# Forgetting attention by pairs of heads on the two halves of TensorE's array

## The reference, cut to what matters

```
q, g = split(h @ w_qg);  q = q * 64 ** -0.5
logits = einsum('bqhd,bkhd->bhqk', q_block, k) + (c_q - c_k)   # float32
logits = where(key_pos <= query_pos, logits, -inf)
p = softmax(logits);  o = einsum('bhqk,bkhd->bqhd', p, v)
y = (o * sigmoid(g)) @ w_out
```

## Time and profile before

| | us |
|---|---|
| median of 3 runs | 2778.18 |
| lowest, highest | 2772.0, 2779.1 |
| profiled execution | 2774.4 |
| its span | 2772.6 |
| PE busy in it | 2685.2 (97%) |
| DVE, ACT, POOL busy | 1536.2, 1021.2, 98.6 |

### The profile page before, as it was taken

The page is one execution under the profiler, slowest core; times in us unless marked ns, Lnnn a source line. Parts: engine busy times, 40 slices in busy tenths (PEclk is TensorE's granted clock), DMA queues, the critical chain, the costliest instruction groups (busy, mean ns, idle before and its releaser), DMA issues. The chain is left out here.

```text
span 2772.6 us, 31166 instructions
## 1 busy us (share of the span) xinstructions
PE 2685.2 (97%) x12382; PEld 2094.1 (76%) x12382; DVE 1536.2 (55%) x2570; ACT 1021.2 (37%) x1588; POOL 98.6 (4%) x124
## 2 busy tenths in 40 slices
PE   8999999999999999999998999999999998999998
PEld 6787688887976656888876876688887765788886
DVE  5455676776255554747465255466653898433432
ACT  4344443334234444434245334323223213322322
POOL 0000000000000000000000000011100110000000
PEclk9999999999999999999999999999999999999999
DMA  5323235542221112333324210266642111233231
GB/s 167 102 81 94 78 119 162 167 149 88 70 85 46 39 46 61 103 95 95 96 69 135 84 61 9 94 194 194 193 146 82 54 46 38 76 99 99 93 98 46
DMA packets 283495, 266.84 MB, mean 96 GB/s; under 512 B 13283, under 2 KB 268567, under 8 KB 283351
## 3 DMA queue, kind: packets, MB, share of 16 engines
q1 hardware_dynamic: 266919, 210.33, 24.7%
q0 software_dynamic: 15024, 54.33, 6.7%
q10 hardware_dynamic: 1408, 0.20, 0.0%
HBM read 262.72 MB, written 2.10 MB: 96 GB/s over the span
## 5 line engine op out<-in xcount | busy, mean ns | idle before, releaser
L481 DVE TENSOR_TENSOR w_lo<-raw,w_hi 128x1024 fp32r<-128x1024 f32 x396 | 482.9, 1224 | 745.8 <-ACT w_hi L476 744.9
L2145 PE MATMUL G<-H_hi,w_hi 128*128 128x512 f32 (+1 forms) x2016 | 812.1, 403 | 15.1 <-DVE H_lo L357 7.9
L476 ACT ACTIVATE w_hi<-raw 128x1024 fp32r<-128x1024 f32 x396 | 417.0, 1056 | 1019.6 <-PE G L2145 911.5
L2145 PE MATMUL G<-H_hi,w_lo 128*128 128x512 f32 (+1 forms) x2016 | 786.4, 390 | 0.0
L2145 PE MATMUL G<-H_lo,w_hi 128*128 128x512 f32 (+1 forms) x2016 | 786.1, 390 | 0.0
L2145 PEld LDWEIGHTS G<-H_hi,w_hi 128*128 128x128 f32 x2016 | 381.3, 189 | 133.9 <-issue 53.2
L2145 PEld LDWEIGHTS G<-H_lo,w_hi 128*128 128x128 f32 x2016 | 381.5, 189 | 83.7 <-issue 9.1
L2145 PEld LDWEIGHTS G<-H_hi,w_lo 128*128 128x128 f32 x2016 | 380.9, 189 | 80.0
L2145 PE MATMUL G<-hid_hi,w_hi 128*128 128x512 f32 x864 | 343.4, 397 | 4.7 <-DVE hid_lo L600 4.7
L2145 PE MATMUL G<-hid_hi,w_lo 128*128 128x512 f32 x864 | 338.1, 391 | 0.0
L2145 PE MATMUL G<-hid_lo,w_hi 128*128 128x512 f32 x864 | 337.9, 391 | 0.0
(11 more groups left out here) (305 smaller groups left out, 2581.5 us busy)
## 6 DMA issues: line engine op xcount, KB each, us to landing
raw<-in_w_ff SPq DMA_DIRECT2D x128, 512.0 KB
mod_w<-in_w_mod POOLq DMA_DIRECT2D x96, 512.0 KB, 4.5
raw<-in_ffn_w_up SPq DMA_DIRECT2D x176, 256.0 KB
raw<-in_ffn_w_down SPq DMA_DIRECT2D x40, 512.0 KB
raw<-in_w_in SPq DMA_DIRECT2D x28, 512.0 KB
raw<-in_mlstm_w_in SPq DMA_DIRECT2D x24, 512.0 KB
raw<-in_kv_w SPq DMA_DIRECT2D x16, 512.0 KB
raw<-in_fox_w_qg SPq DMA_DIRECT2D x16, 512.0 KB
```

Of the source, the lines that this page charges most:

```text
L476: act.activation(w_hi[:, j, :], raw[:, j, :], ACT.Copy).then_inc(hi_done, 1)
L481: dve.tensor_tensor(w_lo[:, j, :], raw[:, j, :], w_hi[:, j, :], ALU.subtract).then_inc(lo_done, 1)
L2145: mm = pe.matmul(G[:, 2 * p + m, 0:n], lw[:, k, ms], rh[:, t, 0:n], start=(t == 0 and q == 0), stop=(t == st["ktiles"] - 1 and q == 2), sk ...
```

## The change

- Two heads (2q and 2q + 1, e = 0 and 1) are worked together: a step n is block b = n % 4 of pair q = n // 4; 32 steps instead of 64.
- `scores(n)`: head e reads partitions 64e to 64e + 63 (as before) and writes bank M0 or M1 by e, not by b. The keys of each head are cut in two pieces (256 + 256 in block 3, 256 + 128 in block 2, 128 + 128 in block 1, one piece in block 0), and the order is piece 0 of head 0, piece 0 of head 1, piece 1 of head 0, piece 1 of head 1. Scores n wait for both logits of step n - 1.
- `values(q)`: the eight products of the pair alternate between the heads, head 0 onto partitions 0 to 63 of M3 and head 1 onto 64 to 127. `output` takes all 128 partitions at once.
- `turn(n, e)` comes two steps behind `scores(n)`; the two of a step have one projection unit between them, and still share bank M2. Scores of the next step stand last in a step.
- Steps 0 to 25 have two projection units each, one at the start and one between the turns. Steps 26 and 27 have none, steps 28 to 31 one unit of `x_out` each, and two more stand between the last turns.
- `row(1)` is issued ahead of the loop; two rows are issued in blocks 0 and 1 of each pair; xN0 holds four rows, both heads are masked in block 3.
- On ACT a step is exponential of head 0, evacuation of head 0 (of step n - 2), exponential of head 1, evacuation of head 1, the row copy, then splits and evacuations of projections. On DVE it is both logits, both scalings of step n - 1, the output, the maskings, then the splits.
- In the diff the three long loops are those of PE, ACT and DVE, in this order.
- The tiles xL, x_row, xN0, xN1 and xPT get new places and packed layouts (only the causal part is held; xPT once instead of twice).

```diff
+        xL = at("xL", 160 * K, [P, 2, 10 * P])
+        xN0 = at("xN0", 176 * K + 128, [P, 4, T])
+        xPT = at("xPT", 188 * K, [P, 24 * P])
...
-            pool.wait_ge(fx["y"], FOX_HEADS)
+            pool.wait_ge(fx["y"], FOX_HEADS // 2)
...
+        FOX_PAIRS = FOX_HEADS // 2
+        FOX_STEPS = TB * FOX_PAIRS
+        WOVEN_STEPS = (8 * 7 - FOX_AHEAD) // 2
+        xl_at = [0, P, 3 * P, 6 * P]
         def units_by(step):
-            return FOX_AHEAD + sum(1 for k in range(8 * 7 - FOX_AHEAD) if 4 * (k // 4) + UNIT_AT[k % 4] <= step)
+            return min(FOX_AHEAD + 2 * (step + 1), 8 * 7)
...
+        def probs(e, b):
+            return xL[:, e, xl_at[b]:xl_at[b] + (b + 1) * P]
+        def turned_probs(e, b):
+            first, pitch = (b * P, 4 * P) if e == 0 else (16 * P - 4 * P * b, 5 * P)
+            return xPT[:, first:first + (b + 1) * pitch].rearrange("p (s m) -> p s m", m=pitch)[:, :, 0:P]
+        def key_probs(e, s):
+            first = 5 * P * s if e == 0 else 5 * P * (3 - s) + (s + 1) * P
+            return xPT[:, first:first + T - s * P]
...
-                if n >= 2:
-                    pe.wait_ge(fx["m"], n - 1)
-                pe.matmul(M[:, b % 2, 0:(b + 1) * P], xQ[hs, h // 2, b * P:b * P + P], xK[hs, h // 2, 0:(b + 1) * P],
-                          start=True, stop=True).then_inc(fx["s"], 1)
+                if n:
+                    pe.wait_ge(fx["m"], 2 * n)
+                half = (b + 1) * HP if b % 2 else (b + 2) // 2 * P
+                for first, end in ((0, half), (half, (b + 1) * P)):
+                    for e in range(2 if end > first else 0):
+                        hs = slice(HP * e, HP * e + HP)
+                        mm = pe.matmul(M[:, e, first:end], xQ[hs, q, b * P:b * P + P], xK[hs, q, first:end],
+                                       start=True, stop=True)
+                mm.then_inc(fx["s"], 1)
...
+                    place = s if e == 0 else b - s
+                    mm = pe.transpose(M[:, 2, place * P:place * P + P], probs(e, b)[:, s * P:s * P + P], ident[:])
...
                 for s in range(TB):
-                    mm = pe.matmul(M[0:HP, 3, s * P:T], xV[:, s, HP * h:HP * h + HP], xPT[h % 2][:, s, s * P:T],
-                                   start=(s == 0), stop=(s == TB - 1), skip_group_check=True)
+                    for e in range(2):
+                        h = 2 * q + e
+                        mm = pe.matmul(M[HP * e:HP * e + HP, 3, s * P:T], xV[:, s, HP * h:HP * h + HP], key_probs(e, s),
+                                       start=(s == 0), stop=(s == TB - 1), skip_group_check=True)
...
+            for n in range(FOX_STEPS):
+                q, b = n // TB, n % TB
+                if n == WOVEN_STEPS:
+                    finish(work)
+                unit(n)
+                if b == 2 and q:
+                    values(q - 1)
+                if n >= 2:
+                    turn(n - 2, 0)
+                unit(n)
+                if n >= 28:
+                    next(outs)
+                if n >= 2:
+                    turn(n - 2, 1)
+                if b < 2 and q < FOX_PAIRS - 1:
+                    row(2 * (q + 1) + b)
+                if n < FOX_STEPS - 1:
+                    scores(n + 1)
+            for n in (FOX_STEPS - 2, FOX_STEPS - 1):
+                for e in range(2):
+                    turn(n, e)
+                    if n < FOX_STEPS - 1:
                         next(outs)
+            values(FOX_PAIRS - 1)
             finish(outs)
...
+            for n in range(FOX_STEPS):
+                q, b = n // TB, n % TB
+                exps(n, 0)
+                if n >= 2:
+                    turned(n - 2, 0)
+                exps(n, 1)
+                if n >= 2:
+                    turned(n - 2, 1)
+                if b < 2 and q < FOX_PAIRS - 1:
+                    row(2 * (q + 1) + b)
+                for _ in range(evacuated_by(n - 1, 3) - taken):
+                    next(work)
+                    taken += 1
+                if n == WOVEN_STEPS:
+                    finish(work)
+                    act.wait_ge(chunk_used, used_after("x_g3"))
+                for t in {26: (0, 1), 27: (2, 3), 28: (4,), 29: (5,)}.get(n, ()):
+                    mixed(t)
...
+            for n in range(FOX_STEPS):
+                q, b = n // TB, n % TB
+                for e in range(2):
+                    logits(n, e)
+                if n:
+                    for e in range(2):
+                        scaled(n - 1, e)
+                if b == 2 and q:
+                    output(q - 1)
+                if b == 3 and q < FOX_PAIRS - 1:
+                    masked(2 * q + 2)
+                    masked(2 * q + 3)
+                for _ in range(evacuated_by(n - 2, 2) - taken):
+                    next(work)
+                    taken += 1
+                if n == WOVEN_STEPS + 1:
+                    finish(work)
+                for t in {27: (0, 1), 28: (2, 3), 29: (4,), 30: (5,)}.get(n, ()):
+                    mixed(t)
```

More of the change, by code:

```diff
@@ new lines, in turned_probs, with scores, turn @@
+        def turned_probs(e, b):
[4 more added lines that the diff above has]
+            return xPT[:, first:first + T - s * P]
+        def fox_pe(pe, linear, linear_units, from_h, squares_behind):
+            def scores(n):
+                q, b = n // TB, n % TB
+                if b == 0 and q % 2 == 0:
+                    wait_read(pe, f"x_q{q // 2}", 0)
+                if n:
+                    pe.wait_ge(fx["m"], 2 * n)
[6 more added lines that the diff above has]
+                mm.then_inc(fx["s"], 1)
+            def turn(n, e):
+                b = n % TB
+                if 2 * n + e:
+                    pe.wait_ge(fx["pt"], 2 * n + e)
+                pe.wait_ge(fx["p"], 2 * n + e + 1)
@@ L1108, in row @@
                     pe.wait_ge(row_c, 5)
-                elif h >= 3:
-                    pe.wait_ge(fx["y"], h - 2)
+                elif h // 2 >= 3:
+                    pe.wait_ge(fx["y"], h // 2 - 2)
                 if h:
@@ L1120, in fox_pe @@
             linear("x_q0", H_hi, H_lo, need=from_h("pre1"))
+            row(1)
             def woven():
@@ L1129, in fox_pe @@
             wait_all_read(pe, "kv_k")
-            scores(0, 0)
+            scores(0)
             next(work)
@@ L1133, in fox_pe, with unit @@
             outs = linear_units("x_out", H_hi, H_lo, need=from_h("fox"), behind=squares_behind("post1"), every=1)
[L1134 to L1151, removed]
-                        next(outs)
[L1153 to L1157, removed]
+            def unit(n):
+                if n < WOVEN_STEPS:
+                    next(work)
[21 more added lines that the diff above has]
+                    if n < FOX_STEPS - 1:
+                        next(outs)
+            values(FOX_PAIRS - 1)
             finish(outs)
@@ L1201, in fox_act, with exps, turned @@
             finish(keys)
[L1203 to L1213, removed]
+            def exps(n, e):
+                b = n % TB
+                act.wait_ge(fx["m"], 2 * n + e + 1)
+                act.activation(probs(e, b), probs(e, b), ACT.Exp, bias=mx[:, b, 2 * e + 1:2 * e + 2], scale=-1.0,
+                               accum_out=rsum[:, b, 2 * e:2 * e + 1]).then_inc(fx["e"], 1)
+            def turned(n, e):
+                q, b = n // TB, n % TB
+                if b == 0 and q:
+                    act.wait_ge(fx["o"], q)
+                act.wait_ge(fx["t"], 2 * n + e + 1)
+                act.activation(turned_probs(e, b), M[:, 2, 0:(b + 1) * P].rearrange("p (s n) -> p s n", n=P),
                                ACT.Copy).then_inc(fx["pt"], 1)
@@ L1232, in fox_act @@
             work, taken = woven(), 0
[L1233 to L1250, removed]
+            for n in range(FOX_STEPS):
+                q, b = n // TB, n % TB
+                exps(n, 0)
[15 more added lines that the diff above has]
+            for e in range(2):
+                turned(FOX_STEPS - 2, e)
             mixed(6)
-            for b in range(1, TB):
-                turned(FOX_HEADS - 1, b)
+            for e in range(2):
+                turned(FOX_STEPS - 1, e)
             mixed(7)
@@ L1323, in scaled, with logits @@
[L1323 to L1327, removed]
+            def logits(n, e):
+                q, b = n // TB, n % TB
+                h, first = 2 * q + e, b * P
+                out, least = probs(e, b), 3.0e38
+                dve.wait_ge(fx["s"], n + 1)
+                if q:
+                    dve.wait_ge(fx["t"], 2 * (n - TB) + e + 1)
+                dve.memset(tok[:, 16 + 4 * e + b:17 + 4 * e + b], 0.0)
+                if b:
+                    link(dve.tensor_tensor_reduce(out[:, 0:first], M[:, e, 0:first], xN0[:, h % 4, 0:first], -1.0, least,
+                                                  ALU.add, ALU.min, mx[:, b, 2 * e:2 * e + 1]))
+                    dve.memset(tok[:, 24 + 4 * e + b:25 + 4 * e + b], 0.0)
```

(33 more changed lines are left out.)

69 lines of the change are left out of this document (25 added, 44 removed).

## The result

| | before | changed |
|---|---|---|
| median of 4 runs each | 2776.68 us | 2738.02 us |
| lowest to highest | 2772.0 to 2779.1 | 2733.85 to 2741.9 |
| profiled execution | 2774.4 us | 2741.9 us |
| its span | 2772.6 us | 2740.1 us |

The ratio is 0.9863, 95% interval 0.9841 to 0.9884: 39 us faster. A second series of the unaltered changed kernel gave 2735.83 (ratio 0.9852, 0.9835 to 0.9868).

A forecast was written before the change was run, and what follows sets the result against it. PE, busy 97% of the span, was taken as the bound. Saving 30.8 us over eight pairs, less 0.6 for waits and 7 at the end, gave 23.2 us off and a median of 2755 us, range 2744 to 2771.

The forecast's parts named there:

- only the second pass of one product overlaps the first of the next: n equal products that alternate take n + 1 pass times: Scores and values on PE: alternating two-pass products of two heads overlap only partly, n + 1 pass times instead of 2n.
- two overlap terms: Per pair of heads, overlap of the halves saves 1.27 us in the scores and 1.71 us in the values.
- Weight loads as a second bound: Scores: if loads can't run beside each other, a pair's streaming takes 3.20 us instead of 2.77; 3.0 was taken.
- The reading of L1422: Products alternating between column halves at 30.9 ns a pass, against 53 alone, were read as two running side by side.
- Turns and projections: PE's transposes and projection products keep their counts; units broken into 8 groups instead of 6 cost 0.1 us a pair.
- Handing over of bank 2: Bank 2 passes to ACT and back within one unit; waits cost 0.1 us a pair, ends 0 and 0.8.
- The end of the attention: From step 26 no unit lies between; some 9.5 idle us against 2.45, so 7 lost, ends 3 and 12.
- the second: Rival: nothing overlaps in scores or values, the end loses less idle time; 2775 us, chance 0.12.
- first: Rival: only column halves overlap, so scores gain only the shape changes; 2765 us, chance 0.15.
- third: Rival: only row halves overlap, exposed value loads eat the values' overlap; 2768 us, chance 0.08.
- the fourth: Rival: the attention's end falls to half clock for all of its 38 us, 12 more; 2767 us, chance 0.06.
- the fifth: Rival: bank 2 becomes the bound, 1.6 us lost in each of 32 steps; slower, 2806 us, chance 0.05.

The follow-up runs named there:

- e1: Changed kernel with both heads of a pair on the same half, so no halves to overlap: 2770.27 us, ratio to before 0.9973.
- e3: Changed kernel with score pieces head by head, both pieces of the first head and then both of the second: 2735.65 us, ratio to before 0.9844.
- e4: Changed kernel with a pair's values head by head, four products of the first and then four of the second: 2747.85 us, ratio to before 0.9891.
- e9: Changed kernel with a pair's values by threes: three products of the first head, three of the second, then one of each: 2749.37 us, one run.
- e10: Changed kernel with a pair's values by twos: two products of the first head, two of the second, then again: 2735.18 us, one run.
- e2: Changed kernel with each head's scores of a step as one product, not cut in two pieces of the keys: 2735.12 us, ratio to before 0.9848.

## Why the prediction was wrong

What bounds the kernel, and that only PE's sum counts, held. So did the terms read from rows: e1 gives 25.13 for a pair without overlap, and 26.54 less my 0.97 for shapes, less the 0.47 found below for turns and projections, is 25.10. The 0.20 once for each group of scores and 0.17 for the values are there unchanged.

The step that failed is "only the second pass of one product overlaps the first of the next: n equal products that alternate take n + 1 pass times". It rested on one assumption, that PE starts passes strictly in order, so that a product's second pass, which waits for its half, also holds up the other head's product behind it. The runs show it wrong: a pass starts as soon as its own half is free if no more than three passes wait ahead of it (`e3`, `e4`, `e9`, `e10`). I also called this counting the bound of the overlap, so that no rival and no sign of being wrong was faster than the forecast. The two overlap terms alone would have made it 2745, at the edge of the range (0.8 + 0.43 a pair, below); the terms of turns, of bank 2 and of the end took it out. By term:

- Scores: I said 3.0 us of streaming in place of 4.27; it is 3.01 - 4 x 0.20 = 2.2. 0.8 a pair too little.
- Values: 2.56 in place of 4.27; it is 2.13. 0.43 too little.
- Weight loads as a second bound (3.20 in the scores): none seen. Twenty-eight loads of 128 columns a pair cost no more than sixteen (`e2` against the changed kernel: 1.06 and 1.07 in the widest step). The Trainium skill's "TensorE: Matmul & The Clock Gate" (Part 3, The mechanism) has the rule that a load overlaps running products only when its row group differs. That doesn't hold in the values here, as I had weighed: both heads' loads are for all rows, and sixteen passes take the 2.30 us of eight. The same section of the Trainium skill also lets a load run ahead into a background weight buffer, which I had left out; the 2.30 us agree with that. The same page's section "Measured speedup vs the span model" gives a pack of tiles the time of one product and some 4 ns for each further one; the 7 ns and the unchanged 2.30 us agree with that, and by it both terms would have come out near what was measured.
- The reading of L1422: I took it as support for my counting. Its mean, 30.9 ns a pass, was no support: in long alternation both countings give the same, and only the ends of a chain differ. Its start could have decided, in the trace before: a narrow window (1503.8 to 1503.9) holds two records, 6 ns apart, where my counting has the second column half wait for the first one's second pass, some 0.1 us later.

```profile
1503.84 0.28 PE L1422 MATMUL G<-rm,sel 128*64 128x64 f32 x2
```

- Turns and projections: I charged 0.1 a pair for two more breaks. The sum of all else, 26.54 - 0.97 - 2.13 - 2.13 = 21.31, leaves 0.47 against 20.84: a gain. Transposes with a projection behind them cost 0.18 less than ahead of scores or a row (0.35 against 0.53), and the projection 0.09 more, four times a pair: 0.36. Summed from start to start over a pair, turns go from 3.04 to 2.28 us and projections from 11.75 to 11.97. I had taken the turns' durations over, without asking how much of them was the change of shape behind them.
- Handing over of bank 2: I took 0.1 a pair, with up to 0.8. No steady turn waits: PE is busy in all of the 20.84 us.

Together 0.8 + 0.43 + 0.57 + 0.1 = 1.9 a pair, 15 over eight pairs. The end of the attention: 7 us lost in my sum, from 2.45 idle to 9.5; it is 6.7 idle (33.10 - 26.39), 4.3 lost. The long stall I put at 4 us is 2.87, at the place and with the releaser I named. The clock at the end: the stretch at half is 6.8 us where there were 10.2; I had let it stand. With 3 for the end and 1 to 2 for the clock, 23 becomes 42 to 43, against 44.2 measured in the attention. In the median 39 to 43 of that are seen.

The errors of the pair's terms all point the same way; none of them made up for another. Of the rivals, e1 disposes of the second and, with the score rows, of the first and third; the fourth expected the half clock for all of the end, which had it for 6.8 of 33 us; the fifth expected waits in every step, and no steady pair has one.

## What to carry to other kernels

In this kernel f32 products that need only half of the array's rows or columns ran two at a time when neighbours in the queue used different halves; the second head of a pair was nearly free, in scores and in values. Strict alternation wasn't needed, but no more than two f32 products (four passes) of the one half could stand ahead of the other's. When a forecast turns on the order in which products start, look at the first records of a chain and not at its mean time. Then price groups by the change of shape around them. And compare the granted clock over many runs before a shortened stage is called slower or faster than its sum: one execution of an unaltered stage can hold 0 or 17 us at half clock.

## What the runs showed of the hardware that I had not expected

- PE starts a pass past others that wait for their half, past three and not past four. Behind its partner it started 7 ns (alternating), 13 (`e3`) and 15 (`e10`) at the head of the chain, and 6 ns behind the first head's third pass (`e9`) and fifth (`e4`, 1.56 us late) where more passes stood ahead of it.
- Row halves and column halves behave alike: 3.01 against 2.93 us for the scores, 2.30 against 2.30 for the values, two heads against one.
- Behind the attention the same code had 48 to 76 us at half clock in ten executions and took 1741.7 to 1754.4 us: 13 us that no edit made.
